# Paged sample attention beside prompt attention on one core: key pages turned by VectorE instead of TensorE, their transfers on GpSimd's queue, every second product on GpSimd

## What is computed

```
z = einsum('bqhd,bkhd->bhqk', q, k) * HEAD_DIM ** -0.5 + bias
log_1m_beta = where(causal, log_sigmoid(-z), 0.0)
tail = cumsum(log_1m_beta, axis=3, reverse=True) - log_1m_beta
w = where(causal, exp(log_sigmoid(z) + tail), 0.0)
out = einsum('bhqk,bkhd->bqhd', w, v)
```

## Time and profile before

| | |
|---|---|
| median of 3 runs | 2828.01 us (2826.99 to 2832.66) |
| profiled execution, its own time | 2821.11 us |
| its span | 2819.6 us |
| busy over the span: PE, DVE, ACT, POOL | 2586.6, 1379.9, 1055.4, 648.4 us |
| prompt and sample attention | about 702 to 1512 us of the span |

### The profile page before, as it was taken

How to read it: one execution, slowest core, us unless ns; L and a number is a source line. 1 busy time by engine, 2 the same in 40 slices (tenths; PEclk the granted TensorE clock), 3 DMA queues, 4 the chain that set the end, 5 groups by cost and what they waited for, 6 DMA issues and landing times. The chain is left out here.

```text
span 2819.6 us, 64656 instructions
## 1 busy us (share of the span) xinstructions
PE 2586.6 (92%) x23589; PEld 1361.0 (48%) x23589; DVE 1379.9 (49%) x2816; ACT 1055.4 (37%) x1938; POOL 648.4 (23%) x918
## 2 busy tenths in 40 slices
PE   6999999996799899899998999789999998899978
PEld 3444444442455445454543555445555554555533
DVE  2151423333678788687886777522222222222228
ACT  2221314121677777687773222122222221122214
POOL 0202020101021211111111222343333333333333
PEclk9999999998899999999999999899999999999989
DMA  9011111126586766767675344399999789999947
GB/s 335 15 61 44 45 45 43 62 85 244 174 271 218 264 234 224 262 213 244 225 262 187 116 140 139 143 261 295 281 301 299 210 257 306 323 309 297 305 134 315
DMA packets 297027, 577.06 MB, mean 205 GB/s; under 512 B 80278, under 2 KB 96727, under 8 KB 292812
## 3 DMA queue, kind: packets, MB, share of 16 engines
q1 hardware_dynamic: 194472, 427.99, 47.4%
q0 software_dynamic: 102016, 146.26, 16.9%
q10 hardware_dynamic: 324, 0.10, 0.0%
HBM read 461.12 MB, written 112.29 MB: 203 GB/s over the span
## 5 line engine op out<-in xcount | busy, mean ns | idle before, releaser
L1253 DVE TENSOR_TENSOR_SCAN left<-leave,left 128x512 f32<-128x512 f32 (+3 forms) x320 | 358.4, 1120 | 134.9 <-ACT leave L1135 134.1
L442 PE MATMUL bank<-xnT,w_in 128*128 128x512 f32 x768 | 330.3, 592 | 0.0
L2056 DVE TENSOR_TENSOR sg<-sg,bank 128x128 f32<-128x128 f32 x160 | 46.0, 288 | 562.5 <-ACT sg L1992 561.3
L2023 PE MATMUL bank<-w,hT 128*32 128x256 f32 x5120 | 297.5, 380 | 1.5 <-issue 1.1
L1056 POOL DMA_DIRECT2D w_out<-in_cache_v x256 | 137.6, 538 | 660.9 <-issue 658.6
L1935 POOL DMA_DIRECT2D rowsP<-xs_d x328 | 218.0, 665 | 200.0 <-DMA rowsP<-xs_d 111.4
L2016 PE MATMUL bank<-w,o_sq 128*32 128x256 f32 x3840 | 218.0, 384 | 30.2 <-DVE o_sq L2051 23.2
L442 PEld LDWEIGHTS bank<-xnT,w_in 128*128 128x128 f32 x768 | 145.6, 190 | 181.8 <-issue 178.9
L1992 ACT ACTIVATE sg<-bank 128x128 f32<-128x128 f32 x160 | 44.4, 278 | 501.2 <-PE bank L2016 501.2
L1619 PE MATMUL bank<-w_out,w 128*128 128x512 f32 x512 | 227.7, 597 | 1.8 <-DVE w L1683 1.8
L442 PE MATMUL bank<-w_in,xnT 128*128 128x512 f32 x512 | 220.4, 592 | 0.0
(11 more groups left out here) (408 smaller groups left out, 3402.1 us busy)
## 6 DMA issues: line engine op xcount, KB each, us to landing
w_out<-in_cache_v POOLq DMA_DIRECT2D x256, 256.0 KB
w_out<-in_cache_k SPq DMA_DIRECT2D x256, 256.0 KB
w<-in_w SPq DMA_DIRECT2D x128, 512.0 KB, 17.4
w<-in_w SPq DMA_DIRECT2D x22, 2048.0 KB, 23.1
oT<-in_w SPq DMA_DIRECT2D x22, 2048.0 KB, 24.2
w_out<-in_w SPq DMA_DIRECT2D x20, 2048.0 KB, 25.7
ys_d<-zeros SPq DMA_DIRECT2D x32, 816.0 KB
ys_d<-y POOLq DMA_DIRECT2D x166, 128.0 KB, 7.8
```

The costliest lines, as they stand in the source:

```text
L442: mm = pe.matmul(ps[:, :], w, m, start=(i == 0), stop=(i == len(parts) - 1))
L1253: dve.tensor_tensor_scan(left[n % 4][:, 0:cols][:, ::-1], leave[n % 4][:, 0:cols][:, ::-1], leave[n % 4][:, 0:cols][:, ::-1], left[n % 4][ ...
L2023: mm = pe.matmul(yb[q * Q:q * Q + Q, u * (XW // 2):(u + 1) * (XW // 2)], hT[:, u, j, :], w2[i][:, j, q * (XW // 2):(q + 1) * (XW // 2)], s ...
```

## The change

Key pages are no longer turned by PE. GpSimd's queue brings each of the 256 pages in one transfer, cut into 4 strips of 128 columns (heads 2s and 2s+1 in strip s) which land on 32 partitions each: 512 pieces of 512 bytes. `k_strips` reuses one of 8 one-page slots as soon as the page in it is turned. DVE turns a page in one instruction of 32 by 32 blocks, 128 by 512 (`k_turn`), straight into `kTs`. The token order inside a page and the order of the head's columns are then permuted, so `keys` reads `kTs` in blocks of 32 columns, the sample queries and new keys are laid out to suit (one more ACT copy, 4 transposes, and 16 small copies in place of 8), and the sample sigmoids put the columns back in order.

SP issues the value pages, 4 per step (`v_pages`), at the ticks at which they were consumed, ahead of the zero fills and loads.

The products of odd items go to GpSimd (`weights` there, counted by `s_wp`); DVE keeps the even ones. ACT copies all turned products out. DVE's start value for items off the diagonal needs no copy: the scan takes one element more (leave is 1.0 there) and the item's old first column as its start.

```diff
+        proj_c = k.sb("proj_c", [P, 512])
...
+                act.wait_ge(s["pje"], 1)
+                act.activation(proj_c[:, :].rearrange("p (c s n) -> p c s n", c=FC, s=STRIPS),
+                               proj[:, :].rearrange("p (s c n) -> p c s n", c=FC, s=STRIPS), ACT.Copy).then_inc(s["pce"], 1)
...
-                dve.tensor_copy(seqs(keep["kT_new"]), part4("k"))
-                for pair in range(H // 2):
-                    for half in range(2):
-                        rows = slice(64 * half, 64 * half + 64)
-                        c0 = (2 * pair + half) * TS
-                        dve.tensor_copy(keep["q_blk"][rows, :, pair, c0:c0 + TS],
-                                        part("q")[rows, pair, :].rearrange("p (b t) -> p b t", b=BS))
+                dve.wait_ge(s["pC"], 1)
+                dve.tensor_copy(keep["kT_new"][:, :, :], part("k", "pC"))
+                for f in range(FC):
+                    for strip in range(STRIPS):
+                        rows = slice(Q * strip, Q * strip + Q)
+                        c0 = (2 * strip + f // 2) * TS
+                        dve.tensor_copy(keep["q_blk"][rows, :, f, c0:c0 + TS],
+                                        part("q", "pC")[rows, f, :].rearrange("p (b t) -> p b t", b=BS))
                 dve.wait_ge(s["sig"], 1)
...
+    PAGES = [(j, i) for j in range(4) for i in range(PPC)]
+    SLOTS, VALUES = 8, (4, 7, 10, 13)
...
-            EVENTS.append((("turn", n - 2), "dve" if (n - 2) % 4 == 0 else "act"))
+            EVENTS.append((("turn", n - 2), "act"))
...
-        if p < 4 * FC and 0 <= unit < NU:
-            EVENTS.append((("k_turn", unit, p), "dve" if p in (3, 7, 11) else "act"))
...
-        kp = [keep["w_out"][:, 0, PPC * i:PPC * i + PPC, :] for i in range(2)]
+        kp = [keep["w_out"][:, 0, i, :] for i in range(SLOTS)]
...
+        def k_page(u, p):
+
+            g = 4 * PPC * u + p
+            return kp[g % SLOTS], s_kp[g % SLOTS], 16 * (g // SLOTS + 1)
+
+        def keys(j, f):
+
+            return kTs[j].rearrange("p f n -> p (f n)").rearrange("p (b f r) -> p f b r", f=FC, r=Q)[:, f]
...
+                def v_pages(g):
+                    u, i = divmod(g, PPC)
+                    if u >= NU:
+                        return
+                    if g >= 2:
+                        sp.wait_ge(s_spv, g - 1)
+                    for j in range(4):
+                        sp.dma_start(vp[g % 2][:, j, :], cache["cache_v"][ds(page(sp, u, j, i), 1)].rearrange("a p n -> (a p) n")).then_inc(s_vp[g % 2], 16)
...
-                for u in range(NU):
-                    for j in range(4):
-                        g = 4 * u + j
-                        if g >= 2:
-                            turned(sp, "k_turn", (g - 2) // 4, 4 * ((g - 2) % 4) + FC - 1)
-                        page(sp, "cache_k", kp[g % 2], s_kp[g % 2], u, j)
...
+                for g in range(2):
+                    v_pages(g)
+                sp.wait_ge(s_set, 1)
+                for n in range(TICKS):
+                    u, p = place(n - 1)
+                    if p in VALUES and 1 <= u <= NU:
+                        v_pages(PPC * (u - 1) + VALUES.index(p) + 2)
+                    if p == 2 * PPC and 1 <= u < NU:
+                        zero_rows(2 * u - 1)
+                    if p == 4 * PPC and 0 <= u < NU:
+                        zero_rows(2 * u)
...
+                def k_strips(g):
+                    u, p = divmod(g, 4 * PPC)
+                    if u < NU:
+                        dst, landed, _ = k_page(u, p)
+                        if g >= SLOTS:
+                            pool.wait_ge(s_kd, g - SLOTS + 1)
+                        pool.dma_start(dst, cache["cache_k"][ds(page(pool, u, *PAGES[p]), 1)].rearrange("a t (s n) -> s (a t) n", n=P)).then_inc(landed, 16)
+
+                def weights(n):
+
+                    cols = item(n)[4]
+                    pool.wait_ge(s_tk, n + 1)
+                    pool.wait_ge(s_sc, n + 1)
+                    pool.tensor_tensor(take[n % 4][:, 0:cols], take[n % 4][:, 0:cols], left[n % 4][:, 1:cols + 1], ALU.mult).then_inc(s_wp, 1)
...
-                for g in range(PPC * NU):
-                    u, i = divmod(g, PPC)
-                    if g >= 2:
-                        pool.wait_ge(s_spv, g - 1)
-                    for j in range(4):
-                        at = (4 * (u // NY) + j) * NPAGES + (NY - 1 - u % NY) * PPC + i
-                        number = pool.value_load(pages[0:1, at:at + 1], min_val=0, max_val=NPHYS - 1)
-                        pool.dma_start(vp[g % 2][:, j, :], cache["cache_v"][ds(number, 1)].rearrange("a p n -> (a p) n")).then_inc(s_vp[g % 2], 16)
+                for g in range(SLOTS):
+                    k_strips(g)
+                for n in range(TICKS):
+                    if n % 2 == 0 and 0 <= n - 1 < N:
+                        weights(n - 1)
+                    u, p = place(n - 1)
+                    if p < 4 * PPC and 0 <= u < NU:
+                        k_strips(4 * PPC * u + p + SLOTS)
...
-                    act.activation(kTs[p // FC][:, p % FC, :], bank("k_turn", u, p)[:, :], ACT.Copy).then_inc(s_ca, 1)
...
+                    in_order = lambda t: t.rearrange("p (i r t) -> p i r t", r=Q, t=STRIPS)
+                    turned_order = lambda t: t.rearrange("p (i t r) -> p i r t", r=Q, t=STRIPS)
+                    act.activation(in_order(s_leave[:, :]), turned_order(z[:, :]), ACT.Sigmoid, scale=-SCALE, bias=nbias[:, 0:1])
+                    act.activation(in_order(s_take[:, :]), turned_order(z[:, :]), ACT.Sigmoid, scale=SCALE, bias=bias[:, 0:1]).then_inc(s_ca, 1)
...
+                def multiplied(n):
+
+                    dve.wait_ge(s_wp if n % 2 else s_w, n // 2 + 1)
+
                 def first(n):
 
                     _, t, c, _, cols = item(n)
-                    if n >= 4:
-                        dve.wait_ge(s_w, n - 3)
                     if c == t // TPG:
+                        if n >= 4:
+                            multiplied(n - 4)
                         dve.memset(left[n % 4][:, cols:cols + 1], 1.0).then_inc(s_in, 1)
+
+                def scanned(n):
+
+                    _, t, c, _, cols = item(n)
+                    dve.wait_ge(s_lv, n + 1)
+                    if c == t // TPG:
+                        dve.wait_ge(s_in, sum(item(m)[2] == item(m)[1] // TPG for m in range(n + 1)))
+                        size, carry = cols, left[n % 4][:, cols:cols + 1]
                     else:
-                        dve.tensor_copy(left[n % 4][:, GRP:], left[n % 4][:, 0:1]).then_inc(s_in, 1)
+                        multiplied(n - 4)
+                        size, carry = GRP + 1, left[n % 4][:, 0:1]
+                    dve.tensor_tensor_scan(left[n % 4][:, 0:size][:, ::-1], leave[n % 4][:, 0:size][:, ::-1], leave[n % 4][:, 0:size][:, ::-1],
+                                           carry, ALU.mult, ALU.bypass).then_inc(s_sc, 1)
...
-                def turn(n):
-
-                    _, t, c, par, cols = item(n)
-                    m = n // 4
-                    turned(dve, "turn", n)
-                    if m >= 2:
-                        dve.wait_ge(s_pv, m - 1)
-                    dve.tensor_copy(wT[m % 2][par][:, 0:cols // P, t % 2, :],
-                                    bank("turn", n)[:, 0:cols].rearrange("p (j q) -> p j q", q=P)).then_inc(s_cd, 1)
...
                 def k_turn(u, p):
-                    turned(dve, "k_turn", u, p)
+                    rows, landed, count = k_page(u, p)
+                    j, i = PAGES[p]
+                    dve.wait_ge(landed, count)
                     if u:
                         turned(dve, "scores", u - 1)
-                    dve.tensor_copy(kTs[p // FC][:, p % FC, :], bank("k_turn", u, p)[:, :]).then_inc(s_cd, 1)
+                    dve.transpose(kTs[j].rearrange("p f n -> p (f n)")[:, i * GRP:i * GRP + GRP], rows).then_inc(s_kd, 1)
 
                 def new_turn(hb):
                     turned(dve, "new_turn", hb)
...
+                for i in range(4):
+                    dve.memset(leave[i][:, GRP:], 1.0)
+                dve.drain()
                 first(0)
                 for n in range(TICKS + 1):
-                    if 0 <= n - 3 < N and (n - 3) % 4 == 0:
-                        turn(n - 3)
                     u, p = place(n - 1)
                     if p == 0 and u in (1, NY + 1):
                         new_turn(u // NY)
                     if p == 0 and u in (NY + 1, NU + 1):
                         out(u // NY - 1)
-                    if p in (3, 7, 11) and 0 <= u < NU:
+                    if p < 4 * PPC and 0 <= u < NU:
                         k_turn(u, p)
-                    if 0 <= n - 1 < N:
+                    if 0 <= n - 1 < N and n % 2:
                         weights(n - 1)
...
+                        scanned(n)
...
-                    pe.wait_ge(s_w, n + 1)
+                    pe.wait_ge(s_wp if n % 2 else s_w, n // 2 + 1)
...
```

(12 more changed lines are left out.)

73 lines of the change are left out of this document (22 added, 51 removed).

## The result

| | before | changed |
|---|---|---|
| median | 2828.01 us (3 runs) | 3067.22 us (3 runs, 3063.30 to 3078.01) |
| ratio | | 1.0849, 95% interval [1.0802, 1.0896] |
| profiled execution, its span | 2821.11, 2819.6 | 3078.01, 3076.5 |
| attention | 702 to 1512 us | 702 to 1750 us |

The change costs 239 us, 8.5%. 2803 was predicted, with 2730 to 2855 as the range: wrong in direction and outside it. Nearly all of the loss lies in the attention, which takes 1048 us in place of 810.

The account below looks back on a forecast made before the run. PE was taken to set the pace, DVE close behind and limiting after the change. DVE's 620 work + 75 turns + 89 idle = 784 us against 810; with 1 us added elsewhere, 2796 profiled, 2803 us median, range 2730 to 2855.

Parts of the forecast that it names:

- That is hidden: Attention's key page transfers: dearer by some 24 us of 810, said to fit in the 30% of engine time free.
- the rival that got 0.05: Key page transfers get dear: decides at 54 ns a packet; at 80 the time is near 3040 us; chance 0.05.
- price of a piece: Key page transfers: a 512-byte packet takes about 27 ns of DMA engine time, a page of 512 of them 14 us.
- Turning a page: DVE turning a key page, 128 by 512: 0.69 us each, 177 us for 256 pages.
- ACT's relief: ACT in the attention: loses 67.9 + 58.3 us of key copies, gains 80 product copies of 0.55, stays near 520 us.
- transfer instruction: GpSimd issuing a key page: 0.61 us idle plus 0.97 us for 512 pieces, 404 us for 256 pages.
- 75 us were taken for turns: DVE scans and GpSimd products reading SBUF: strict turns taken, so scans wait 75 us in all.
- 620 were summed: DVE's work in the attention: 644 us, less 201 removed, plus 177 for turning key pages.
- where key pages stood: Value pages on SP's queue take the key pages' place, behind the same zero fills and loads; if late, 10 us or so.
- 89 were predicted: DVE's idle time after: start and end 20, pauses behind sample scores 42, diagonal items 22, small waits 5 us.
- loop gets longer: Rival: the attention's engine chain slows, by late odd products, PE's lower clock or pages turned at 1.2 us: 2835 us; chance 0.18.
- The clock: Sign of a wrong prediction: PE's clock drops in the middle of the attention phase; no size given.

Follow-up runs that it names:

- e12: Changed kernel, each key page as 512 pieces of 512 bytes but with 128 as slowest dimension, rows to their own partitions: 2831.10 us, ratio 1.0024.
- e1: Changed kernel, but each key page comes as 128 plain rows of 2 KB instead of 512 pieces of 512 bytes, same queue: 2823.83 us, ratio 1.0012.
- e5: Changed kernel with key pages as plain rows of 2 KB and all 320 products on DVE: 2813.59 us, ratio 0.9946.
- e14: Changed kernel, half the key pages as strips in four transfers each on GpSimd's queue, half plain on SP's, turned by PE; products on DVE: 2823.60 us, 0.9990.
- e8: Kernel before with only the 513-element scan, which starts from the item's old first column without a copy: 2820.89 us, ratio 0.9981.
- e2: Changed kernel with keys on SP's queue, each page as four transfers, one per strip, and values on GpSimd's: 3228.46 us, ratio 1.1426.
- e13: Changed kernel, strips as four transfers a page, three on SP's queue, the fourth and the values on GpSimd's, all products on DVE: 3049.86 us, ratio 1.0811.
- e3: Changed kernel with queues exchanged: strips, one transfer a page, on SP's queue, values on GpSimd's: 3421.71 us, ratio 1.2109.
- e7: Changed kernel with each key page as two strips, 256 pieces of 1 KB, slowest dimension 2: 3117.22 us, ratio 1.1028.
- e10: Changed kernel, key pages as 128 whole rows of 2 KB in another row order, slowest dimension 4: 2913.01 us, ratio 1.0316.

## Why the prediction was wrong

**"That is hidden"**, said of the dear transfers, is the step that failed, in the rival that got 0.05. Its price of a piece held (14 us a page, e12: 13.4). What it lacked was that the transfer's slowest dimension, the 4 strips, limits the engines that carry it. All of the trace's page transfers have 128 rows there, so no row could show it, and I priced only the pieces and the third dimension. Its reckoning failed too: it asked only whether the 30% of the engines' time that was free would be used up, at 54 ns a packet or 27.7 us a page. The page came to 24.6 us, below that, and the phase still became 238 us longer: pages on both queues land late (18.5 and 12.1 us after issue, 5.4 and 4.6 in e1). The Trainium skill states the rule for the number of engines on the page that the prediction cited for the cost of issuing, in another section. That the rival's time, 3040 us, came near was luck: it stood for 80 ns a packet.

**Turning a page** (0.69 us) and **ACT's relief** (528.7 us busy against 520) came out as worked. The **transfer instruction** (1.57 us against 0.61 + 0.97) did so by luck: with the same 512 pieces and 128 as slowest dimension it takes 0.77 (e12), and the rest came with the 4. In e1, without the strips, the product on GpSimd is 1.13 us (1.2 predicted).

**DVE and GpSimd.** 75 us were taken for turns. In e1 DVE is busy 688 us where 620 were summed: 68 us. That term was right in size, though it shows as longer scans and not as gaps. By the Trainium skill (SBUF — State Buffer, Who interferes with whom) a DVE instruction with two SBUF inputs and a GpSimd instruction that reads SBUF exclude each other for the whole instruction. e1 comes near it where they meet: two thirds of the overlap on the scans, and on the 9 of DVE's 112 wide products that met one of GpSimd's all of it (5.1 us beside, 5.2 longer); spans on GpSimd are rough.

**The second error** lies in e1, where 25 us should have been left and none was. The last scans of the kernel before and of e1, the load of the first half of the output weights in both, and what PE waits for behind e1's attention:

```profile
1501.96 1.27 DVE L1253 TENSOR_TENSOR_SCAN left<-leave,left 128x512 f32<-128x512 f32 x1
1463.30 1.70 SPq L1012 DMA_DIRECT2D w_out<-in_w_out  x1
```

```profile
1485.32 1.27 DVE L1201 TENSOR_TENSOR_SCAN left<-leave,left 128x513 f32<-128x513 f32 x1
1483.29 0.57 SPq L1038 DMA_DIRECT2D w_out<-in_w_out  x1
PE bank L1645 <- DMA w_out<-in_w_out: 8.7, 2, 5.3
PE bank L1645 <- DVE w L1709: 7.4, 1, 7.4
```

The scans of e1 end at 1486.6 us and those of the kernel before at 1503.2: 17 us were won (in e5 23, in e14 11). But from there to the end e1 takes 1328.6 us and the kernel before 1316.4. The load of the weights was issued 40 us before the last scan ended, and now 3 us before, behind the last value pages on SP's queue, so PE stands 16 us at the start of the next phase. The prediction put the value pages "where key pages stood" and did not ask what stands behind them: key pages are done with a unit earlier. e5 and e14 (1331.5 and 1330.5 us) and the changed kernel (1336.0) show the same, while e8, e2 and e13, whose value pages are on GpSimd's queue, take 1315 to 1316. Two others lie between: e3, with values on GpSimd's queue, and e7, with values on SP's, both 1322. No run moves this load by itself, so its 12 to 15 us are read from the waits and not shown by an experiment. These are all profiled executions; e1's is the fastest of its eight, 7 us below their median.

Within the attention 9 us of the predicted 26 are missing. Up to 1495 us, as far behind the last scan as 1512 is in the kernel before, DVE is busy 687 us of 793 and idle 106, where 89 were predicted:

```profile
702.00:1495.00 793.00, 637.79 (x4170) 290.39 (x4170) 686.52 (x937) 532.06 (x1054) 303.87 (x421) 0.94 0.71 233
```

PE's waits for products rose from 25.7 us to 116 (82.0 for DVE's, 34.4 for GpSimd's), as PE's own group of turns in e1 has it:

```profile
L1343 PE MATMUL tb<-ident,take 128*128 128x128 f32 x1088 | 185.0, 294 | 117.5 <-DVE take L1209 82.0 <-POOL take L1087 34.4 <-ACT wT L1108 0.4
```

This is part of the "loop gets longer" rival, which gave 2835 at a chance of 0.18; e1's 2824 is near it, but more of the missing time is the late load. The sum kept DVE's pauses at the ends and behind the sample scores and nearly dropped the rest; 17 us more of it stayed. In a loop of four engines what one is relieved of it partly waits.

**The clock**, named as a sign of failure, did fall: 0.84 over the stretch, 0.62 where value pages are late. It goes with the stalls: in e1, without them, it is 0.94.

**Still open:** why data packets on both queues take longer, and value pages on the other queue land 12 us after issue in place of 4.6 (e1), when transfers beside them run on 4 engines; the further packets themselves are short, 21.7 ns on average. And why 4 engines cost 3.2% with rows and 8.5% with pieces, beyond that a page holds the engines 19.6 and 24.6 us.

## What to carry to other kernels

Before costing a transfer that cuts rows into blocks, write out both access patterns and look at the slowest dimension, not only at the size of a piece: 512 pieces of 512 bytes cost 0.2% with 128 there and 8.5% with 4. If the layout needs such a dimension, one transfer per block mends it (e14, for half of the pages), but then each queue's issue rate is the budget (0.9 to 1.15 us each here). When transfers change queues, look also at what now stands behind them: a load of weights that came 37 us later, seen from the last scan, took back most of what e1 had won. And where four engines pass work round and the first is 89% busy, work taken from another is worth little (e8: 25 us of instructions, 10 of busy time, 5 of the program): measure such a part alone first.

## What the runs showed that was not expected

- On GpSimd's queue a transfer that few engines carry brings further packets of 4 bytes for each piece, as many as give each other engine its like number: 192 a page with 4 engines, 448 with 2. They are 6 points of the DMA share; it rises while GB/s fall (0.93 and 179 against 0.70 and 233) because the data packets of both queues take longer.
- The same on SP's queue shows no such packets and a share of 0.2 to 0.3, but a page needs 3.47 us and holds the queue as long (e3).
- GpSimd's transfer instruction grows with the narrowness and the pieces: 0.56 us for plain rows, 0.69 with 4 (e10), 0.77 for 512 pieces (e12), 1.57 for both, 2.1 with 2 (e7).
- With GpSimd's products in the loop a scan takes 1.48 us on average in place of 1.28: 1.83 where a product lies beside it for 0.6 us or more, 1.27 where none does.
